# A hybrid layer and a mixer block on one core: next queries in the tail of each neighbourhood pass, context rows over the query buffers, the out operand split early, the final norm by halves

## The reference, cut to what matters

```python
# first block: neighbourhood attention and a gated convolution, 1024 tokens (16 x 64), 256 context rows
h  = rmsnorm(x, norm_g) * (1 + scale) + shift
hc = rmsnorm(ctx, norm_g) * (1 + scale_c) + shift_c
q, k, v, za, u, bg, cg, zc = split(h @ w_in)          # 8 heads of 64
q, k = rmsnorm(heads(q), q_norm_g), rmsnorm(heads(k), k_norm_g)
kc, vc = split(hc @ w_in[:, keys and values])
# latent scores: roped q, k in a window of 8 rows x 16 columns, plus bias; context scores: plain q with kc
attn = softmax([q_rot k_rot + bias, q kc]) @ [v, vc] * silu(za)
conv = bg * short_conv(cg * u) * silu(zc)
x = x + gate * (concat([attn, conv]) @ w_out)
# second block
x = x + hybrid_mixer(rmsnorm(x))                      # differential and forgetting attention
x = x + memory_cross_attention(rmsnorm(x), rmsnorm(mem))
x = x + square(relu(rmsnorm(x) @ w1)) @ w2
return rmsnorm(x, g_final)
```

## Time and profile before

| | us |
|---|---|
| median of 3 runs | 2747.57 (2745.29 to 2747.58) |
| profiled execution | 2748.74 |
| its span, first to last instruction | 2746.9 |
| PE busy in the span | 2587.7 (94%) |
| DVE busy | 1107.1 (40%) |
| ACT busy | 803.1 (29%) |
| POOL busy | 765.7 (28%) |

### The profile page before, as it was taken

How to read it: one execution, slowest core, us unless ns; L and a number is a source line. 1 busy time by engine, 2 the same in 40 slices (tenths; PEclk the granted TensorE clock), 3 DMA queues, 4 the chain that set the end, 5 groups by cost and what they waited for, 6 DMA issues and landing times.

```text
span 2746.9 us, 34507 instructions
## 1 busy us (share of the span) xinstructions
PE 2587.7 (94%) x12792; PEld 2128.9 (78%) x12792; DVE 1107.1 (40%) x1758; ACT 803.1 (29%) x1326; POOL 765.7 (28%) x492
## 2 busy tenths in 40 slices
PE   7899999999899999999999899997999999999997
PEld 2677877888787878778787688885788888888886
DVE  3553555545545544445444553444242121121123
ACT  3343444434412443344433521232021010010110
POOL 1131314122247222222222133323233333333331
PEclk9899999999999999999999999998999999999998
DMA  8412213030345222211222134210211111111111
GB/s 310 145 57 78 64 48 99 19 115 31 132 131 171 71 71 67 70 60 61 70 66 70 69 122 168 92 47 31 77 61 48 51 46 47 52 46 46 53 46 69
DMA packets 68165, 218.25 MB, mean 79 GB/s; under 512 B 21180, under 2 KB 21436, under 8 KB 63172
## 3 DMA queue, kind: packets, MB, share of 16 engines
q1 hardware_dynamic: 45316, 123.67, 14.2%
q10 hardware_dynamic: 22720, 92.81, 10.3%
...
## 4 chain that ended last, share of the span: by engine, by line
PE 74%; issue 7%; DVE 6%; ACT 5%; DMA 4%; POOL 1%; SPq 1%; ACTq 0%; DVEq 0%; POOLq 0%
PE ps L1869 14%; PE ps L1870 13%; PE ps L1872 13%; PE ps L1856 8%; PE ps L1857 8%; PE ps L1858 8%; DMA raw<-in_w_stream_dram 2%; PE ps L2262 1%; DMA ada<-in_w_ada_dram 1%; PE ps L2090 1%; PE ps L2066 1%; DVE stage L1679 1%; SPq L380 1%; ACT pt_hi L671 1%; ACT p_hi L968 1%
## 5 line engine op out<-in xcount | busy, mean ns | idle before, releaser
L410 POOL CAST w_hi<-raw 128x1024 fp32r<-128x1024 f32 x192 | 208.3, 1085 | 1753.1 <-issue 783.6
L1856 PE MATMUL ps<-act_hi,w_hi 128*128 128x512 f32 x1168 | 471.5, 404 | 12.3 <-POOL w_lo L412 9.0
L412 POOL TENSOR_TENSOR w_lo<-raw,w_hi 128x1024 fp32r<-128x1024 f32 x192 | 470.8, 2452 | 15.4
L1857 PE MATMUL ps<-act_lo,w_hi 128*128 128x512 f32 x1168 | 461.1, 395 | 5.6 <-issue 5.6
L1858 PE MATMUL ps<-act_hi,w_lo 128*128 128x512 f32 x1168 | 461.5, 395 | 0.0
L1869 PE MATMUL ps<-act_hi,w_hi 128*128 128x512 f32 x1008 | 396.4, 393 | 9.9 <-DVE act_lo L1208 5.3
L1870 PE MATMUL ps<-act_lo,w_hi 128*128 128x512 f32 x1008 | 394.8, 392 | 0.0
L1872 PE MATMUL ps<-act_hi,w_lo 128*128 128x512 f32 x1008 | 312.2, 391 | 0.0
L1856 PEld LDWEIGHTS ps<-act_hi,w_hi 128*128 128x128 f32 x1168 | 222.5, 190 | 53.2 <-POOL w_lo L412 9.2
L1858 PEld LDWEIGHTS ps<-act_hi,w_lo 128*128 128x128 f32 x1168 | 222.3, 190 | 49.3
L1857 PEld LDWEIGHTS ps<-act_lo,w_hi 128*128 128x128 f32 x1168 | 223.1, 191 | 45.5 <-issue 6.5
...
## 6 DMA issues: line engine op xcount, KB each, us to landing
raw<-in_w_stream_dram SPq DMA_DIRECT2D x192, 512.0 KB, 3.5
...
```

Of the source, the lines that this page charges most:

```text
L410: nc.gpsimd.tensor_copy(w_hi[:, s, :, :], raw[:, s, :, :]).then_inc(S["w_hi"], 1)
L412: nc.gpsimd.tensor_tensor(w_lo[:, s, :, :], raw[:, s, :, :], w_hi[:, s, :, :].bitcast(F), ALU.subtract).then_inc(S["w_split"], 1)
L1856: nc.tensor.matmul(out, wh, xh, start=start, stop=False)
L1857: nc.tensor.matmul(out, wh, xl, start=False, stop=False)
```

## The change

- `hc_hi` and `hc_lo` lie over the query buffers (`qp`, `qr`) instead of those of the probabilities. ACT issues their reload in unit 14, once all scores of the pass are made.
- The tail of each looped pass takes the next pass's first half of q, its context keys and its second half of q, around the eight transposes. For the first pass these stand ahead of the loop. In the head the sums of k come first, then both halves of the next tile, and `half_turn(0)` stands behind the second of them. ACT takes k's roots ahead of the context keys' copies.
- The tile for u goes by halves, the second behind the first two scores, with three steps of the convolution behind it. ACT makes unit 0's exponentials before it copies u. The last pass has a table of steps of its own, in which the halves of the convolution end inside units and units 14 and 15 have three steps each.
- Parts 0 to 2 of the out operand are split before or around the last product of pass 4; the first two tiles of the out projection go by halves of k.
- The final norm goes by two halves of 512 tokens: half of the last tile, then the other, with the sums of the first half inside it. The output leaves in sixteen DMAs of 256 KB instead of eight of 512 KB.

```diff
-        st = ExitStack()
-        hc_hi = alloc(st, "hc_hi", [P, KT, C], R)
-        hc_lo = alloc(st, "hc_lo", [P, KT, C], R)
-        st.close()
...
+        st = ExitStack()
+        hc_hi = alloc(st, "hc_hi", [P, KT, C], R)
+        hc_lo = alloc(st, "hc_lo", [P, KT, C], R)
+        st.close()
         qp = alloc(st1, "qp", [P, 2, T], R)
...
-        CONV_STEPS = [4, 4, 3, 3, 2, 4, 4, 3, 3, 2, 4, 4, 4, 4, 0, 0]
-        HALF_TAKEN = {1: [0], 4: [1], 6: [2], 9: [3], 11: [4], 13: [5]}
+        CONV_STEPS = {False: [1, 4, 3, 3, 2, 4, 4, 3, 3, 2, 4, 4, 4, 4, 0, 0],
+                      True: [1, 3, 3, 3, 2, 4, 3, 3, 3, 2, 3, 3, 3, 3, 3, 3]}
+        HALF_TAKEN = {False: {1: [0], 4: [1], 6: [2], 9: [3], 11: [4], 13: [5]},
+                      True: {2: [0], 5: [1], 7: [2], 10: [3], 13: [4], 15: [5]}}
+        TAPS = {False: {4: [1], 5: [0, 2]}, True: {5: [1], 6: [0, 2]}}
...
-            for k in range(KT):
-                sp.wait_ge(S["y_ready"], k + 1)
-                sp.dma_start(y_t[:, k, :], res[:, k, :]).then_inc(S["y_out"], 16)
-            sp.wait_ge(S["y_out"], 16 * KT)
+            for c in range(2):
+                x = slice(c * BANK, (c + 1) * BANK)
+                for k in range(KT):
+                    sp.wait_ge(S["y_ready"], KT * c + k + 1)
+                    sp.dma_start(y_t[:, k, x], res[:, k, x]).then_inc(S["y_out"], 16)
+            sp.wait_ge(S["y_out"], 32 * KT)
...
                 evacuated(tC, tD, 0)
+                head_rms(0)
                 act.wait_ge(S["tile_done"], t0 + 1)
                 nc.scalar.activation(kraw, bank(6, 0, C), ACT.Copy)
                 nc.scalar.activation(ksq, bank(6, 0, C), ACT.Square).then_inc(S["ck_rms"], 1)
-                head_rms(0)
                 act.wait_ge(S["tile_done"], t0 + 2)
...
-                act.wait_ge(S["tile_done"], t0 + 5)
-                nc.scalar.activation(cv_x, ps[:, 4 * BANK:6 * BANK], ACT.Copy).then_inc(S["cv_u"], 1)
...
                 exp_unit(0)
+                act.wait_ge(S["tile_done"], t0 + 5)
+                nc.scalar.activation(cv_x, ps[:, 4 * BANK:6 * BANK], ACT.Copy).then_inc(S["cv_u"], 1)
                 for u in range(16):
...
+                    if u == 14 and not last_pair:
+                        act.wait_ge(S["na_scores"], 16 * i + 16)
+                        act.wait_ge(S["hc_saved"], 32)
+                        act.dma_start(hc_hi[:, :, :].bitcast(F), hc_dram[:, 0, :, :]).then_inc(S["hc_in"], 16)
+                        act.dma_start(hc_lo[:, :, :].bitcast(F), hc_dram[:, 1, :, :]).then_inc(S["hc_in"], 16)
...
+                if last_pair:
+                    act.wait_ge(S["tile_done"], T_OUT)
+                    mixed_hi(0)
+                    mixed_hi(1)
                 other_half(7)
-                if again:
-
-                    act.wait_ge(S["hc_saved"], 32)
-                    act.dma_start(hc_hi[:, :, :].bitcast(F), hc_dram[:, 0, :, :]).then_inc(S["hc_in"], 16)
-                    act.dma_start(hc_lo[:, :, :].bitcast(F), hc_dram[:, 1, :, :]).then_inc(S["hc_in"], 16)
+                if last_pair:
+                    mixed_hi(2)
+                    return
                 act.wait_ge(S["conv_done"], i + 2)
 
                 note()
                 act.dma_start(conv_dram[:, bass.ds(i, 1), :].rearrange("p o t -> p (o t)"), cv_y
                               ).then_inc(S["conv_out"], 16)
...
             act.wait_ge(S["pair_done"], 5)
             act.dma_start(res[:, 4:7, :], conv_dram[:, 0:3, :]).then_inc(S["rows_in"], 16)
-            act.wait_ge(S["tile_done"], T_OUT)
-            split_hi(act_hi, S["rows_in"], cv_y)
+            mixed_hi(3)
+            act.wait_ge(S["rows_in"], 32)
+            for k in range(4, 7):
+                mixed_hi(k)
+            act.wait_ge(S["conv_done"], 5)
+            mixed_hi(7, cv_y)
...
+            def final_square_half(c):
+                x = slice(c * BANK, (c + 1) * BANK)
+                act.wait_ge(S["mlp_acc"], 34 + c)
+                if c == 0:
+                    act.wait_ge(S["acc_done"], 8 * r + 6)
...
+            final_square_half(0)
+            final_rms(0)
+            final_square_half(1)
+            final_rms(1)
...
@@ -1416,13 +1460,24 @@
                 evacuate(7)
                 dve.wait_ge(S["na_out"], 8 * i + 8)
                 nc.vector.tensor_tensor(tD, tD, tB, ALU.mult).then_inc(S["na_tail"], 1)
+                if last_pair:
+                    dve.drain().then_inc(S["lin_evac"], 2)
+                    mixed_lo(0)
+                    mixed_lo(1)
                 dve.wait_ge(S["na_tail"], 4 * i + 4)
                 dve.wait_ge(S["na_ot"], i + 1)
                 note()
                 nc.vector.tensor_tensor(res[:, bass.ds(i, 1), :].rearrange("p o t -> p (o t)"),
                                         ps[:, 4 * BANK:6 * BANK], tD, ALU.mult).then_inc(S["pair_done"], 1)
...
+            with dve.Fori(0, 3) as i:
+                mix_pair(i, False)
+            mix_pair(3, True)
+            for k in range(2, 7):
+                mixed_lo(k)
+            mixed_lo(7, cv_y)
...
+            last_half(0)
+            last_square(0)
+            final_rstd(0)
+            last_half(1)
+            dve.wait_ge(S["rstd_spread"], r)
+            final_scale(0, 0)
+            last_square(1)
+            final_scale(0, 1)
+            final_scale(0, 2)
+            final_rstd(1)
+            for k in range(3, KT):
+                final_scale(0, k)
+            dve.wait_ge(S["rstd_spread"], r + 1)
             for k in range(KT):
...
+                final_scale(1, k)
...
+            def context_keys(i):
+                pe.wait_ge(S["hc_in"], 32 * i + 32)
+                project(0, 6, hc_hi, hc_lo, C, ready=filled("ctx")).then_inc(S["tile_done"], 1)
+
+            tile_ready(T_ATT + 1)
+            pe.wait_ge(S["ada_step"], 3)
+            project_half(1, 2, 0)
+            context_keys(0)
+            project_half(1, 2, 1).then_inc(S["tile_done"], 1)
...
-                tile_ready(t0 + 1)
-                pe.wait_ge(S["ada_step"], 3)
-                project_half(1, 2, 0)
-
-                pe.wait_ge(S["pair_done"], i + 1)
-                pe.wait_ge(S["hc_in"], 32 * i + 32)
-                project(0, 6, hc_hi, hc_lo, C, ready=filled("ctx")).then_inc(S["tile_done"], 1)
...
                 head_ss(0, tD, 0)
-                project_half(1, 2, 1).then_inc(S["tile_done"], 1)
+                tile_ready(t0 + 2)
+                pe.wait_ge(S["pair_done"], i + 1)
+                project_half(0, 4, 0)
                 pe.wait_ge(S["ck_rms"], 2 * i + 1)
                 nc.tensor.matmul(bank(6, C, 2 * C), bd64, ksq, start=True, stop=True).then_inc(S["ck_ss"], 1)
                 head_spread(0, tD, 0)
-                tile_ready(t0 + 2)
-                project_half(0, 4, 0)
                 head_ss(1, tB, 2)
+                project_half(0, 4, 1)
                 half_turn(0, kh, 0)
-                project_half(0, 4, 1)
                 pe.wait_ge(S["conv_done"], i + 1)
                 project(0, 7, hc_hi, hc_lo, C).then_inc(S["tile_done"], 1)
                 head_spread(1, tB, 2)
...
-                project(0, 4, act_hi, act_lo, T).then_inc(S["tile_done"], 1)
+                project_half(0, 4, 0)
...
                 scores(0)
                 scores(1)
-                done = 0
+                project_half(0, 4, 1).then_inc(S["tile_done"], 1)
+                conv_steps(0, 3)
+                done = 3
...
-                    conv_steps(done, CONV_STEPS[u])
-                    done += CONV_STEPS[u]
+                    conv_steps(done, CONV_STEPS[last_pair][u])
+                    done += CONV_STEPS[last_pair][u]
...
+                if not last_pair:
+                    tile_ready(t0 + 9)
+                    project_half(1, 2, 0)
                 pe.wait_ge(S["na_tail"], 4 * i + 3)
                 for t in range(NT):
                     last = nc.tensor.transpose(ps[:, 4 * BANK + t * P:4 * BANK + (t + 1) * P],
                                                tC[:, t * P:(t + 1) * P], ident)
                 last.then_inc(S["na_ot"], 1)
+                if not last_pair:
+                    pe.wait_ge(S["na_out"], 8 * i + 8)
+                    context_keys(i + 1)
+                    project_half(1, 2, 1).then_inc(S["tile_done"], 1)
...
-            linear_pair("out", T_OUT, "mix", 0)
+            for ks in (range(0, 4), range(4, 8)):
+                for s in range(2):
+                    if ks[0] == 0:
+                        tile_ready(T_OUT + s)
+                        pe.wait_ge(S["lin_evac"], s + 1)
+                    last = project(s, 2 * s, act_hi, act_lo, T, ks, filled("mix"), ks[0] == 0, ks[0] > 0)
+                    if ks[0]:
+                        last.then_inc(S["tile_done"], 1)
...
+            tile_ready(N_TILES - 1)
+            pe.wait_ge(S["mlp_acc"], 32)
+            output_half(0, range(KT)).then_inc(S["half_done"], 1)
+            output_half(1, range(4))
```

(5 more changed lines are left out.)

152 lines of the change are left out of this document (107 added, 45 removed).

## The result

The changed kernel takes 2754.57 us (median of 8 runs, 2752.7 to 2759.27) against 2746.37 for the kernel before (8 runs, 2744.07 to 2749.73). The ratio is 1.003, with a 95% interval of 1.0019 to 1.0041: slower, by 8.2 us. The forecast was 2745.8 and no change. The measured time lies just inside the stated range (to 2755), but slower by more than the 0.2% that I had called no change, and at the price of the second rival (2754.7).

The account below looks back on a forecast made before the run. TensorE, working 94% of the span, was taken as the bound, so only its idle or low-clock time pays. Terms A to H summed to -1.8 us: 2746.9 on the profiled execution, 2745.8 against the median; range 2732 to 2755.

Parts of the forecast that it names:

- second rival: Last pass's waits for the convolution's bank decide, activation queued behind an exponential: 12 us, kernel 2754.7; chance 0.12.
- F: Units of the last pass: five bank waits cost 6.0 us, steps in units 14 and 15 fill 2.9: +3.1.
- C: Head 0's sums to q's spreading: unchanged chain leaves TensorE a 6.2 us wait; only the last pass gains: -1.7.
- G: Last pass's output matmuls to the out projection: early operand splits shrink the wait from 6.72 to 5.1 us: -1.6.
- D: Behind the new wait at q's spreading: lower clock costs 2.4 us in each of four passes: +9.6.
- first rival: The clock holds behind the 6.2 us wait, or the chain shortens: 2736.2 us, faster; chance 0.30.
- A: First pass to q's spreading: k's spreading now follows the third weight tile's wait, so q's moves to 141.3: +7.2.
- E: First unit, q's turn to unit 1's transposes, four passes: halves of u cover the wait for exponentials: -9.4.
- H: Final norm, last weight tile's start to the end: halves of tokens cut 36.30 us to 27.3: -9.0.
- B: Last output matmul to head 0's sums, three turns: half projection more work, as much idle time lost: 0.
- third rival: The branch at the new loop's end is not covered by queued matmuls: 6.8 us more, 2752.6; chance 0.10.

Follow-up runs that it names:

- Experiment 1: The changed kernel with the last pass's convolution-step tables put back as in the looped passes, halves ending at a unit's end; 2742.14 us, ratio 0.9988.
- Experiment 6: Kernel tail with DVE reading the convolution's bank ahead of the low probabilities for the last pass's first four halves; 2718.56 us, ratio 0.9898.
- tail: The changed kernel with PE's old order at the heads and ends of the neighbourhood passes, early reload and last-pass tables kept; 2722.35 us, ratio 0.9908.
- both: The changed kernel with both the old order at pass heads and ends and the old last-pass tables; 2709.51 us, run again on another chip 2714.54.
- mixed: Kernel both, but with q's first half and the context keys kept at the end of the preceding pass; 2711.93 us, ratio 0.9868.
- tab: Kernel of Experiment 1: the changed kernel with only the last pass's convolution-step tables put back; 2742.14 us, ratio 0.9988.
- fill: Kernel tab with the first half of the v tile put ahead of q's spreading; 2740.92 us, ratio 0.9975.
- experiments 9 and 8: Kernel both with the first unit as before the change (9: 2719.69 us), and with the final norm and output DMAs whole again (8: 2723.66 us).

## Why the prediction was wrong, point by point

**F failed, and most of the miss is there.** Of the 12.4 us between the forecast's sum and the measured one, F has 8.4 and C 4.8. The prediction priced a wait inside a unit by the engines that read the bank ("each for one ScalarE activation (0.60), perhaps its table load (1.28) and one VectorE product (0.69)", 1.2 us each, five times), and it let 2.9 us of idle time be filled by the steps moved into units 14 and 15. Measured were 1.7, 2.7, 2.0, 1.2 and 3.0 us, 10.6 in sum, 2.1 each. Experiment 1 shows the table to be the cause, 12.4 us with what it cost G. Experiment 6 shows what the price left out in the first four waits: the read's place in DVE's line, behind the low probabilities. With the read in front they are 0.9 us each, under the price. Three of the waits also left the clock lower (0.94 over the stretch, 0.98 before), and the steps in the last units filled nothing, since the tail then waited 2.4 us for the arithmetic of a half that ended in unit 15. Step by step: +11.5 for +3.1. This is the second rival in place, size (12) and decision point (an average wait of about 2.1), though not in its reason: it had the activation behind an exponential, and in the first four waits it was DVE's line.

**C was right in kind and off in size.** The hole is where and what it was said to be: 7.3 us for 6.2, four times, with the copy of the roots as releaser. The step said that "the chain of VectorE and ScalarE is unchanged". It is 1.0 us longer (k's spreading to q's 19.24 us in all four passes, for 18.24 before in passes 2 to 4; before, pass 1 has the wait for the third tile there). One instruction makes it:

```profile
295.79 2.21 DVE L1320 TENSOR_TENSOR kl<-res,kh 64x1024 fp32r<-64x1024 f32 x1 [2.19 <-ACT kh L583]
```

```profile
293.21 1.29 POOL L416 CAST w_hi<-raw 128x1024 fp32r<-128x1024 f32 x1 [2.41 <-PE ps L1971]
294.58 2.35 POOL L418 TENSOR_TENSOR w_lo<-raw,w_hi 128x1024 fp32r<-128x1024 f32 x1
```

DVE's subtraction took 1.22 us before, and takes 1.22 in tail, both and mixed; here, in tab too, it takes 2.21 (fill: 2.27), and it lies beside POOL's split of the next tile: POOL's subtraction ends at 296.93, and DVE's ends 1.07 us behind that, at 298.00. The Trainium skill, page "SBUF — State Buffer", section "SBUF: two separate sides", says that a VectorE operation with two inputs in SBUF and a GpSimd operation that reads SBUF share a pair of ports as a lock for a whole instruction, so that the later one waits for the earlier one's end; these rows agree with it (2.21 is 1.14 of waiting and 1.07 of work). So do others of this trace, in the last section. The split starts when PE releases a slot, at the end of the context values; with the turn of k behind the half projection and the chain behind the sums, the two now meet. In pass 2 the clock was lower ahead of k's spreading as well (9.4 us for 7.7). The hole itself, and that it follows from work taken out of the head, is shown by tail (no such wait) and by fill (the work put back further on, nothing gained). +3.1 for -1.7.

**D was right in kind, and a little too dear.** The clock granted behind the hole is 0.79 in the stretch of pass 2, where it was 1.00 before, and PE worked without a pause in it. 7.5 us for 9.6. It needs the hole: in tail, with the order undone, the stretch is 8.2, 7.5, 7.5 and 7.8 us as before. The first rival (the clock holds) is out.

**A, E and H** came within 1 us of their numbers (+8.0 for +7.2, -9.2 for -9.4, -9.4 for -9.0). For E and H experiments 9 and 8 show the cause (10.1, and 8 to 10 us). A is right in kind, and its 0.8 is the longer chain of C; but that the number is so close is in part luck, for the third weight tile sets this point, and with the old order it lies between 131.0 and 136.2 us in eight profiles, with the new one between 139.5 and 142.1 in three.

**G** depends on where one counts from. From the tail's transposes it is -2.4 for -1.6, but the 2.4 us that these transposes waited stand in F. From the last output matmul, which is how the prediction defines G, the changed kernel gained nothing on before (7.02 and 6.94): the last pass's table took it. With the old table it is -2.9 (tab). No run took the early split or the halves of k by themselves.

**B had the right sum and hid the finding.** +0.5 for 0, and two of the three tails have the 14.8 us of work that was forecast (14.85 and 14.77). But against the old order with the early reload the moved work costs about 13, and the early reload gains 10 to 13. The prediction gave the early reload no term and put the idle time down to VectorE's tail, the branch and the reload together, without asking what each is worth alone. It also read the idle time wrong: in passes 1 and 2 PE did not wait for the context operand, and the matmuls behind the pause ran at the lower clock (12.50 us busy in pass 1 against 9.41 in both). And the reload moved by more than the two units' 8 us: it is issued 12 to 13 us earlier, measured against the last output matmul (in tail `hc_lo` goes out at 232.68 and lands at 241.09, ahead of the transposes at 245.01). The early reload is a gain by itself, and the order takes it back.

**The third rival** (the branch) is out as a cost of 6.8: of the taken branches' 3.9 and 4.8 us one wait of 1.0 us on "issue" ahead of k's sums is all that PE's rows show. The rule of the Trainium skill (page "Runtime: NRT & Kernel Launch", section "Instruction fetch mechanics"), that a taken branch to a place outside the fetch window waits for a fetch, agrees with the branch rows of this kernel and of before (3.3 to 4.8 us each); the rows of mixed, in the last section, have taken branches of 0.2 us. For the time of the kernel the rule didn't decide.

The chances: 0.20 stood on slower, 0.12 on the case that came. F's own bounds (0 to 2.6 us for each of five waits) are 13 us apart. That is more than the 7 us between the forecast and the first time that counts as slower (2753.1), so this one term could decide the case, and did.
